# Two reorderings around the attentions of a transformer kernel: a gate's bank, a vector engine's order, four weight splits

## The chip, the cores and the metric

One core of one Trainium2 chip runs the whole program. The metric is the device time of one execution in microseconds. TensorE multiplies, VectorE (DVE) and ScalarE (ACT) work on tiles in SBUF and read the results of TensorE from eight PSUM banks of 128 x 512 float32, GpSimd (POOL) does a few small roots, and SyncE (SP) issues the transfers of the weights. Every engine works through its own instructions in order; they meet at semaphores only.

## The reference

Two transformer blocks on one sequence of 512 positions, width 1024, in float32. The first has a mixer of two halves (a gated linear attention and a latent attention with softmax), an MLP and a gated projection:

```python
o_g = gla_chunked(q_g, k_g, v_g, log_a)
o_g = rms_norm(o_g, gla_out_norm[i]).reshape(B, S, GLA_WIDTH) * jax.nn.silu(g_r)
o_m = mla_attention(q_m, k_m, v_m).reshape(B, S, MLA_WIDTH)
h = h + jnp.concatenate([o_g, o_m], axis=-1) @ w_out[i]
```

The second has a pooling mixer, a convolutional feed-forward network, a chunked attention of 16 heads, and the network again:

```python
qkv = h @ w_qkv
q, k, v = jnp.split(qkv, 3, axis=-1)
q = head_rmsnorm(q.reshape(B, S, N_HEADS, HEAD_DIM), q_norm)
k = head_rmsnorm(k.reshape(B, S, N_HEADS, HEAD_DIM), k_norm)
s = jnp.einsum('bqhd,bkhd->bhqk', qc, kb) * scale + bias[None]
p = jax.nn.softmax(s, axis=-1)
```

## The kernel before

**Products.** Each float32 product is made of three products of the faster kind: high part by high part, high by low, low by high (`triple`, L584 to L586, and `triple_t`, L590 to L592). So every unit of weights (128 x 2048) is loaded into a buffer `RAW` by SP, rounded into its high part `WH` by ACT (L1289, the split) and its low part `WL` is the difference, made by DVE (L1677). One unit of the first attention (`MIXED`, the first of the output projection) is split in four quarters on either engine (ACT L1420, DVE L1684), placed into steps of the attention.

**The first attention** (`tensor_program` from L771, `vector_program` from L1994) is a loop of 13 steps that each engine writes out in its own order. In step i TensorE makes scores of step i into banks 0 and 1 (L842), turns the weights of step i-2 into banks 4 and 5 (L852), multiplies the values of step i-3 into bank 6 (L867), turns heads (L771), then does some chunks of the gate projection (`gate_part`; the table `GATED` says how many in each step; 8 chunks are one tile, three products each), and last a level of the linear attention into banks 7 and 3 (L827). All four tiles of the gate go through bank 2, which DVE frees when it moves the tile into `gsil` (L2008). In steps 11 and 12 TensorE makes the states (`states`), for the second half of the heads into banks 0 and 1, and the output projection (`attended`, L896) follows.

DVE does in each step, in order: the finished gate tile, the level that is kept (L1929), the division of the last step's weights (L1975, L1980), the largest score of this step (L1991, L1997), in some steps the low part `LM` of the values (L2025, waits for ACT's `OM`), then the products with the decays (`decayed`) and the next decays' exponents (`decay`), and in steps 7 to 10 a quarter of `MIXED`.

**The second attention** is written out by one planner, `attend_order`, from which all engines take their steps. For each of the blocks of q and k TensorE multiplies the rows (`product`), two halves of the sum for each of four row groups q. After the second half ACT moves the result out of its bank and squares it (`z`, L1627, L1632), DVE sums and averages the squares (L2287, L2290), POOL takes the root (L2420), DVE scales the rows (`scale`, L2295, L2298), and two groups later TensorE turns them (`turn`, L1206) and ACT copies the turned tile out of bank 2 into `qTa` or `kTa` (L1637). The results of `product` go through banks 0 and 1 in turn, so the next but one product waits for ACT's `z`. The steps `high` (ACT's split of a unit, L1289) and `low` (DVE's, L1677) are placed by the same planner; the fourth of a block's two splits is placed at row group 2, second half, ahead of the turn:

```python
if done == 1:
    out.append(("sums", 5))
if (q, half) == (2, 1):
    high(u + 3)
if to_turn and to_turn[0][0] <= done - 3:
    out.append(("turn", *to_turn.pop(0)[1]))
```

The other split of a block, `high(u + 2)`, is placed at row group 1, first half, ahead of the product.

Of the kernel before, what the change touches and what calls it, by code (L numbers as in the profile page):

```python
# [15 lines left out]
P = 128  # L16
# [431 lines left out]
def attend_order():  # L448

    out, split, to_scale, to_turn = [], [], [], []
    pairs = [(0, 0), (1, 0), (0, 1), (1, 1), (2, 0), (3, 0), (2, 1), (3, 1)]
    groups = [(blk, q, half) for blk in BLOCKS for q, half in pairs]
    done = n = 0

    def high(u):
        out.append(("high", u))
        split.append(u)

    def low():
        while split:
            out.append(("low", split.pop(0)))

    def group():
        nonlocal done, n
        blk, q, half = groups[done]
        u = UNIT["qkv", 2 * blk]
        if (q, half) == (1, 0):
            high(u + 2)  # L470
        out.append(("product", blk, half, q))
        if done == 1:
            out.append(("sums", 5))
        if (q, half) == (2, 1):
            high(u + 3)
        if to_turn and to_turn[0][0] <= done - 3:
            out.append(("turn", *to_turn.pop(0)[1]))
        if half:
            if blk >= 4:
                out.append(("v", blk, q))  # L480
            else:
                out.append(("z", blk, q, n))
                to_scale.append((done, (blk, q, n)))
                n += 1
        while to_scale and to_scale[0][0] <= done - 1:
            at, piece = to_scale.pop(0)
            out.append(("scale", *piece))
            to_turn.append((at, piece))
        done += 1

    def project(m, i):
        if m % 4 == 0 and i == 0:
            high(UNIT["wo", 0] + m // 4 + 2)
        out.append(("part", m, i))

    for _ in range(20):
        low()
        group()
    steps, last = len(ATTEND), 11
    parts, tail = [(m, i) for m in range(8) for i in range(2)], steps + 2 - last  # L500
    for s in range(steps + 3):
        if 0 <= s - 1 < steps:
            out.append(("norm", s - 1))
        if s < steps:
            out.append(("scores", s))
        if 0 <= s - 2 < steps:
            out.append(("turned", s - 2))
        if s < steps:
            out.append(("largest", s))
        low()  # L510
        if 0 <= s - 3:
            out.append(("values", s - 3))
            if (s - 3) % 5 in (2, 4):
                out.append(("output", ATTEND[s - 3][0][0]))
        if s < steps:
            out.append(("weights", s))
        if s <= last:
            while done < 20 + 28 * (s + 1) // (last + 1):
                low()
                group()  # L520
        else:
            for m, i in parts[16 * (s - last - 1) // tail:16 * (s - last) // tail]:
                project(m, i)
                if i == 0 and m > 0:
                    out.append(("add", m - 1))
    out.append(("add", 7))
    return out
# [20 lines left out]
HEADS = {0: ((0, 2), (0, 3)), 1: ((1, 2), (1, 3)), 3: ((0, 4), (0, 5)), 4: ((1, 4), (1, 5)),  # L548
         5: ((0, 6), (0, 7)), 6: ((1, 6), (1, 7))}
LEVEL_AT = {1: 4, 2: 5, 3: 6, 4: 8, 5: 9, 6: 10}  # L550
GATED = {-1: 1, 0: 2, 1: 2, 2: 3, 3: 3, 4: 2, 5: 3, 6: 2, 7: 3, 8: 2, 9: 1, 10: 4, 11: 4}
STEPS1 = 10


def level_at(s):

    return next((lv for lv in LEVEL_AT if LEVEL_AT[lv] == s), None)
# [8 lines left out]
def tensor_program(k, e):  # L566
# [11 lines left out]
    def in_bank(b, *name):  # L578
        k.where[name] = b
        return MM.mark(*name)  # L580

    def triple(o, a, c, h, l, first, last):

        e.matmul(o, a, h, start=first, stop=False)  # L584
        e.matmul(o, a, l, start=False, stop=False)  # L585
        return e.matmul(o, c, h, start=False, stop=last)  # L586
# [188 lines left out]
    def gate_part(i):  # L775

        first = sum(GATED[x] for x in GATED if x < i)
        for n in range(first, first + GATED[i]):
            h, c = divmod(n, 8)
            u = UNIT["gr", h // 2]  # L780
            a, l = split_view(k, u, 8)
            cols = slice(h % 2 * P, h % 2 * P + P)
            if c == 0:
                w.wait_ge(WLO(u), *free[2])
            t = triple(bank[2][:, :], a[:, c, cols], l[:, c, cols], AH[:, c, :], AL[:, c, :], c == 0, c == 7)
            if c == 7:
                t.then_inc(*in_bank(2, "gr", h))
                free[2] = [DVE("gr", h)]
                MM.also("unit", u)

    def states(j):

        bs = ((3, 7), (0, 1))[j]
        w.wait_ge(ACT("kd", j))
        for c in (0, 2, 4, 6, 1, 3, 5):
            b = bs[c % 2]
            r0 = 64 * (c % 2)
            if c < 2:
                w.wait_ge(*free[b])
            for hh in range(2):  # L800
                h = 2 * j + hh
                t = e.matmul(bank[b][64 * hh:64 * hh + 64, (c // 2) * P:(c // 2 + 1) * P],
                             k.kd[r0:r0 + 64, c // 2, j * P + 64 * hh:j * P + 64 * hh + 64],
                             k.gv[r0:r0 + 64, c // 2, h * GV:(h + 1) * GV], start=True, stop=True, skip_group_check=True)
            if c in (5, 6):
                t.then_inc(*MM.mark("state", j, c % 2))
        free[bs[0]], free[bs[1]] = [DVE("state", j, 6)], [DVE("state", j, 5)]
# [86 lines left out]
    def attended(m):  # L894

        u = UNIT["wout", m // 4]  # L896
        a, l = split_view(k, u, 4)
        cols = slice(m % 4 * P, m % 4 * P + P)
        b = (3, 2, 0, 1)[m % 4]
        w.wait_ge(WLO(u), *free[b])  # L900
        for c in range(4):
            w.wait_ge(DVE("ol", 4 + c))
            t = triple(bank[b][:, :], a[:, c, cols], l[:, c, cols], k.OM[c][:, :], k.LM[c][:, :], c == 0, c == 3)
        t.then_inc(*in_bank(b, "res", 1, m))
        free[b] = [DVE("x", 1, m)]
        MM.also("unit", u)
# [757 lines left out]
def vector_program(k, e):  # L1664
# [291 lines left out]

    def chain(j):

        bs = ((3, 7), (0, 1))[j]
        for c in range(7):  # L1960
            o = bank[bs[c % 2]][:, (c // 2) * P:(c // 2 + 1) * P]
            w.wait_ge(MM("state", j, 0), MM("state", j, 1)) if c else w.wait_ge(MM("state", j, 0))
            if c == 0:
                w.wait_ge(MM("gr", 3))
                t = e.tensor_copy(k.ST[:, j, 0, :], o)
            else:
                w.wait_ge(DVE("state", j, c - 1), ACT("el"))
                t = e.scalar_tensor_tensor(k.ST[:, j, c, :], k.ST[:, j, c - 1, :], k.el[:, j, c:c + 1], o, MUL, ADD)
            t.then_inc(*DVE.mark("state", j, c))
# [13 lines left out]
    def largest(i):  # L1983
# [13 lines left out]
            t = e.scalar_tensor_tensor(k.st1[:, y:y + 2, x, 1], k.st1[:, y:y + 2, x, 0], -1.0, k.rn[:, 0, r:r + 2], MUL, MUL)  # L1997
        t.then_inc(*DVE.mark("neg1", i))

    zeros = cst[:, C_ZERO:C_ZERO + 1]  # L2000
    last()
    for i in range(STEPS1 + 3):
        h = gate_ends(i - 1)
        if h is not None:
            w.wait_ge(MM("gr", h))
            if h == 2:
                w.wait_ge(MM("level", 5, 1, 1))
            e.tensor_tensor(k.gsil[:, h, :], bank[2][:, :], rb[:, :], MUL).then_inc(*DVE.mark("gr", h))  # L2008
        if i == STEPS1 + 2:
            chain(0)  # L2010
        lv = level_at(i - 1)
        if i in (3, 4):
            keep(0, i - 3)
        elif lv:
            for j in range(2):
                keep(lv, j)
        if 0 <= i - 1 < STEPS1:
            divided(i - 1)
        if i < STEPS1:
            largest(i)  # L2020
        s = i - 3
        if s >= 0 and s % 5 in (2, 4):
            p = ATTEND[s][0][0]
            w.wait_ge(ACT("oh", 4 + p))
            e.tensor_tensor(k.LM[p][:, :], bank[6][:, :], k.OM[p][:, :].bitcast(F), SUB).then_inc(*DVE.mark("ol", 4 + p))  # L2025
        if level_at(i + 1):
            decayed(level_at(i + 1))
        if level_at(i + 2):
            decay(level_at(i + 2))
        if i == 0:  # L2030
            w.wait_ge(ACT("elast"), MM("gv", 1, 3))
            e.tensor_tensor(k.kt[0][:, :, :], k.gk[:, :, :], k.dd[:, :, :], MUL).then_inc(*DVE.mark("kdec"))
            split(9)
        if i == LEVEL_AT[6] + 1:
            w.wait_ge(ACT("efirst"))
            e.tensor_tensor(k.dd[:, :, :], k.gq[:, :, :], k.dd[:, :, :], MUL).then_inc(*DVE.mark("qdec"))
        if 7 <= i <= 10:
            quarter(MIXED, i - 7)

# [584 lines left out]
```

## Time and profile before

| | |
|---|---|
| median of 3 runs | 1654.26 us (1652.44, 1654.26, 1654.32) |
| profiled execution, its own time | 1654.58 us |
| its span, first to last instruction | 1652.8 us |
| TensorE busy | 1644.8 us (100% of the span as the page rounds it), 8124 products |
| DVE busy | 935.8 us (57%) |
| ACT busy | 615.6 us (37%) |
| POOL busy | 84.2 us (5%) |
| DMA | 94 GB/s mean, 25.4% of 16 engines' span for the weights' queue |
| TensorE's granted clock | 0.999 of full speed |

The chain that ended last is TensorE for 96% of the span. The first attention lies at about 95 to 182 us, the projection behind it runs to about 230 us, and the second attention lies at about 1043 to 1262 us.

### The profile page before, as it was taken

Reading aid. Unit: us, or ns where it says so; the run is one execution under the profiler, and the core shown is the slowest. Engines: PE = TensorE matmul, PEld = TensorE weight load, DVE = VectorE, ACT = ScalarE, POOL = GpSimd, SP = SyncE. Lnnn points to the kernel's source line nnn. Section 1 sums busy time; section 2 is a strip of 40 time slices with the busy share of each in tenths; the row PEclk is TensorE's granted clock in tenths of the full one; section 3 lists DMA queues with packets and bytes.
Section 4 is the critical chain, followed back from the end, with each engine's and each line's share of the span. In section 5 each row is a group of like instructions: output and inputs, shape, how many; then the busy total and the mean of one; then the engine's idle time right before and its main releaser. Section 6 shows DMA issues by size and latency. Waiting matters only on the chain.

```text
span 1652.8 us, 19172 instructions
## 1 busy us (share of the span) xinstructions
PE 1644.8 (100%) x8124; PEld 1341.9 (81%) x8124; DVE 935.8 (57%) x1379; ACT 615.6 (37%) x828; POOL 84.2 (5%) x80
## 2 busy tenths in 40 slices
PE   9999999999999999999999999999999999999999
PEld 7877878888888888888888888877777888888887
DVE  6797664434343546576456457546655577366353
ACT  5476444333232336433222223455655333122120
POOL 1300001000000000000000000311200100000000
PEclk9999999999999999999999999999999999999999
DMA  5210227445452521222322222322221222232311
GB/s 186 102 49 27 102 77 130 128 89 110 84 136 80 124 103 52 77 103 102 126 79 102 102 83 96 126 77 78 98 75 52 77 102 103 102 102 89 110 63 70
DMA packets 27909, 155.93 MB, mean 94 GB/s; under 512 B 3696, under 2 KB 5120, under 8 KB 11952
## 3 DMA queue, kind: packets, MB, share of 16 engines
q1 hardware_dynamic: 26352, 149.84, 25.4%
q0 software_dynamic: 1328, 4.86, 5.0%
q8 instruction: 64, 1.05, 0.3%
q14 instruction: 21, 0.17, 0.0%
q10 hardware_dynamic: 144, 0.00, 0.0%
HBM read 149.98 MB, written 4.72 MB: 94 GB/s over the span
## 4 chain that ended last, share of the span: by engine, by line
PE 96%; DVE 2%; ACT 1%; POOL 0%; DMA 0%; issue 0%; SPq 0%; DVEq 0%
PE bank L584 26%; PE bank L586 26%; PE bank L585 26%; PE bank L590 3%; PE bank L592 3%; PE bank L591 3%; PE bank L1218 1%; PE bank L1228 1%; PE bank L1244 1%; PE bank L842 1%; PE bank L827 1%; PE bank L1104 0%; PE bank L1206 0%; PE bank L771 0%; PE bank L867 0%; PE bank L606 0%
## 5 line engine op out<-in xcount | busy, mean ns | idle before, releaser
L584 PE MATMUL bank<-AH,WH 128*128 128x512 f32 (+1 forms) x1150 | 451.5, 393 | 1.5 <-DVE gsil L2008 1.4
L586 PE MATMUL bank<-AH,WL 128*128 128x512 f32 (+1 forms) x1150 | 447.8, 389 | 0.0
L585 PE MATMUL bank<-AL,WH 128*128 128x512 f32 (+1 forms) x1150 | 447.6, 389 | 0.0
L1677 DVE TENSOR_TENSOR WL<-RAW,WH 128x2048 fp32r<-128x2048 f32 (+1 forms) x133 | 298.5, 2247 | 192.7 <-ACT WH L1289 192.7
L1289 ACT ACTIVATE WH<-RAW 128x2048 fp32r<-128x2048 f32 (+1 forms) x133 | 248.3, 1871 | 259.3 <-PE bank L586 240.3
L584 PEld LDWEIGHTS bank<-AH,WH 128*128 128x128 f32 (+1 forms) x1150 | 215.5, 187 | 49.1 <-issue 2.4
L586 PEld LDWEIGHTS bank<-AH,WL 128*128 128x128 f32 (+1 forms) x1150 | 215.5, 187 | 45.9
L585 PEld LDWEIGHTS bank<-AL,WH 128*128 128x128 f32 (+1 forms) x1150 | 215.6, 187 | 45.6 <-issue 1.0
L584 PE MATMUL bank<-HH,WH 128*128 128x512 f32 x608 | 239.6, 394 | 0.0
L586 PE MATMUL bank<-HH,WL 128*128 128x512 f32 x608 | 238.4, 392 | 0.0
L585 PE MATMUL bank<-HL,WH 128*128 128x512 f32 x608 | 236.0, 388 | 0.0
L1707 DVE TENSOR_TENSOR X<-X,bank 128x512 f32<-128x512 f32 x112 | 76.6, 685 | 196.5 <-PE bank L586 196.3
L586 PEld LDWEIGHTS bank<-HH,WL 128*128 128x128 f32 x608 | 114.1, 188 | 26.8
L585 PEld LDWEIGHTS bank<-HL,WH 128*128 128x128 f32 x608 | 114.1, 188 | 25.5
L584 PEld LDWEIGHTS bank<-HH,WH 128*128 128x128 f32 x608 | 114.3, 188 | 22.8
L1598 ACT ACTIVATE t2s<-t2s,par 128x512 f32<-128x512 f32 x44 | 31.9, 724 | 186.7 <-DVE t2s L2253 186.7
L590 PE MATMUL bank<-WH,AH 128*128 128x512 f32 x224 | 90.0, 402 | 0.0
L592 PE MATMUL bank<-WH,AL 128*128 128x512 f32 x224 | 87.5, 391 | 0.0
L591 PE MATMUL bank<-WL,AH 128*128 128x512 f32 x224 | 87.3, 390 | 0.0
L1603 ACT ACTIVATE HH<-cvs 128x512 fp32r<-128x512 f32 x44 | 27.8, 632 | 126.0 <-DVE cvs L2259 126.0
L1518 ACT ACTIVATE t2s<-t1s 128x512 f32<-128x512 f32 x32 | 20.2, 632 | 97.4 <-DVE t1s L2148 97.4
L1296 ACT ACTIVATE sq<-X 128x512 f32<-128x512 f32 x49 | 30.9, 630 | 65.6 <-DVE X L1707 61.6
(306 smaller groups left out, 1746.0 us busy)
## 6 DMA issues: line engine op xcount, KB each, us to landing
RAW<-in_W SPq DMA_DIRECT2D x124, 1024.0 KB, 4.8
RAW<-in_W SPq DMA_DIRECT2D x9, 768.0 KB, 4.1
X<-in_XT SPq DMA_DIRECT2D x16, 256.0 KB, 5.8
ev_scratch<-ev POOLq DMA_DIRECT2D x16, 160.0 KB, 7.5
Gb<-ev_scratch SPq DMA_DIRECT2D x16, 128.0 KB, 2.9
out<-X SPq DMA_DIRECT2D x8, 256.0 KB, 2.0
Gb<-ev_scratch SPq DMA_DIRECT2D x16, 112.0 KB, 2.6
RAW<-in_W SPq DMA_DIRECT2D x2, 512.0 KB, 5.3
```

The source lines that it names most:

```text
L584: e.matmul(o, a, h, start=first, stop=False)
L585: e.matmul(o, a, l, start=False, stop=False)
L586: return e.matmul(o, c, h, start=False, stop=last)
L590: e.matmul(o, h, a, start=first, stop=False)
L591: e.matmul(o, h, c, start=False, stop=False)
L592: return e.matmul(o, l, a, start=False, stop=last)
L1289: e.activation(k.WH[SLOT_OF[u]][:, 0:n], k.RAW[RAW_OF[u]][:, 0:n], AF.Copy).then_inc(*WHI.mark(u))
L1296: e.activation(k.acc if j == 0 else sq[(j - 1) % 2][:, :], src, AF.Square).then_inc(*ACT.mark("sqr", n, j))
L1598: e.activation(t2s[i][:, :], t2s[i][:, :], AF.Silu, bias=par[:, PC_CB + 22 * l + m:PC_CB + 22 * l + m + 1]).then_inc(*ACT.mark("silu", l, m))
L1603: e.activation(k.HH[m % NH][:, :], k.cvs[i][:, :], AF.Copy).then_inc(*ACT.mark("hh", name, m))
L1677: e.tensor_tensor(k.WL[j][:, 0:n], k.RAW[RAW_OF[u]][:, 0:n], k.WH[j][:, 0:n].bitcast(F), SUB).then_inc(*WLO.mark(u))
L1707: e.tensor_tensor(X[:, m, :], X[:, m, :], src, ADD).then_inc(*DVE.mark("x", n, m))
```

## The change

In the first attention: the fourth tile of the gate (h = 3) goes into bank 0 in place of bank 2; the second half's states go into banks 2 and 1 in place of 0 and 1; the banks of the output projection are (0, 3, 2, 1) in place of (3, 2, 0, 1); `GATED` gives the stretch ahead of step 0 two chunks in place of one, and step 2 two in place of three; on DVE the third gate tile (h = 2) is moved out behind the division instead of at the start of its step, the low part `LM` comes behind `decayed` and `decay`, and the quarters 0 to 3 of `MIXED` are in steps 7, 10, 11, 11 in place of 7, 8, 9, 10. In the second attention the planner places the turn ahead of `high(u + 3)`; the two trade places wherever a turn is due there. No arithmetic changes.

```diff
         if done == 1:
             out.append(("sums", 5))
+        if to_turn and to_turn[0][0] <= done - 3:
+            out.append(("turn", *to_turn.pop(0)[1]))
         if (q, half) == (2, 1):
             high(u + 3)
-        if to_turn and to_turn[0][0] <= done - 3:
-            out.append(("turn", *to_turn.pop(0)[1]))
...
-GATED = {-1: 1, 0: 2, 1: 2, 2: 3, 3: 3, 4: 2, 5: 3, 6: 2, 7: 3, 8: 2, 9: 1, 10: 4, 11: 4}
+GATED = {-1: 2, 0: 2, 1: 2, 2: 2, 3: 3, 4: 2, 5: 3, 6: 2, 7: 3, 8: 2, 9: 1, 10: 4, 11: 4}
...
-            cols = slice(h % 2 * P, h % 2 * P + P)
+            cols, b = slice(h % 2 * P, h % 2 * P + P), 0 if h == 3 else 2
             if c == 0:
-                w.wait_ge(WLO(u), *free[2])
+                w.wait_ge(WLO(u), *free[b])
...
-        bs = ((3, 7), (0, 1))[j]
+        bs = ((3, 7), (2, 1))[j]
...
-        b = (3, 2, 0, 1)[m % 4]
+        b = (0, 3, 2, 1)[m % 4]
...
+    def gate_out(h):
+        w.wait_ge(MM("gr", h))
+        if h == 2:
+            w.wait_ge(MM("level", 5, 1, 1))
+        e.tensor_tensor(k.gsil[:, h, :], bank[where["gr", h]][:, :], rb[:, :], MUL).then_inc(*DVE.mark("gr", h))
...
+        if h is not None and h != 2:
+            gate_out(h)
...
             divided(i - 1)
+        if h == 2:
+            gate_out(h)
         if i < STEPS1:
             largest(i)
+        if level_at(i + 1):
+            decayed(level_at(i + 1))
+        if level_at(i + 2):
+            decay(level_at(i + 2))
         s = i - 3
         if s >= 0 and s % 5 in (2, 4):
...
-        if level_at(i + 1):
-            decayed(level_at(i + 1))
-        if level_at(i + 2):
-            decay(level_at(i + 2))
...
-        if 7 <= i <= 10:
-            quarter(MIXED, i - 7)
+        for x in {7: (0,), 10: (1,), 11: (2, 3)}.get(i, ()):
+            quarter(MIXED, x)
```

## Rows read from the trace of the kernel before

**Rows 1.** Waits of TensorE over the run: total us, times, longest.

```profile
PE bank L584 <- DVE gsil L2008: 1.4, 1, 1.4
...
PE bank L1206 <- ACT kTa L1637: 0.6, 1, 0.6
PE bank L842 <- ACT kT L1412: 0.6, 1, 0.6
PE bank L842 <- DVE st L1991: 0.4, 1, 0.4
...
PE bank L584 <- DVE ST L1968: 0.3, 1, 0.3
```

**Rows 2.** Timeline of TensorE, two neighbouring gate chunks: start us, us, instruction.

```profile
169.26 0.39 PE L584 MATMUL bank<-AH,WH 128*128 128x512 f32 x1
...
169.95 0.39 PE L584 MATMUL bank<-AH,WH 128*128 128x512 f32 x1
```

**Rows 3.** Timeline of DVE in the first attention, steps 7 to 10.

```profile
152.13 0.69 DVE L2025 TENSOR_TENSOR LM<-bank,OM 128x512 fp32r<-128x512 f32 x1 [3.00 <-ACT OM L1448]
...
161.31 0.69 DVE L1684 TENSOR_TENSOR WL<-RAW,WH 128x512 fp32r<-128x512 f32 x1
...
167.73 0.68 DVE L2008 TENSOR_TENSOR gsil<-bank,rb 128x512 f32<-128x512 f32 x1
```

**Rows 4.** Timelines of SP, ACT and DVE: the second unit of the output projection.

```profile
172.97 0.33 SPq L2443 DMA_DIRECT2D RAW<-in_W  x1
...
181.73 1.91 ACT L1289 ACTIVATE WH<-RAW 128x2048 fp32r<-128x2048 f32 x1
...
185.65 2.28 DVE L1677 TENSOR_TENSOR WL<-RAW,WH 128x2048 fp32r<-128x2048 f32 x1
```

**Rows 5.** Timeline of ACT in the second attention, first place of the exchange.

```profile
1054.85 1.91 ACT L1289 ACTIVATE WH<-RAW 128x2048 fp32r<-128x2048 f32 x1
1057.56 0.60 ACT L1637 ACTIVATE qTa<-bank 128x512 f32<-128x512 f32 x1 [0.81 <-PE bank L1206]
1058.06 0.68 ACT L1627 ACTIVATE qn<-bank,r 128x512 f32<-128x512 f32 x1
```

**Rows 6.** Timelines of DVE, POOL and TensorE behind the first place.

```profile
1060.24 2.28 DVE L1677 TENSOR_TENSOR WL<-RAW,WH 128x2048 fp32r<-128x2048 f32 x1
...
1064.05 0.69 DVE L2295 TENSOR_TENSOR qn<-qn,rn 128x512 f32<-128x512 f32 x1 [0.73 <-POOL rn L2420]
1064.78 0.69 DVE L2298 TENSOR_TENSOR qn<-qn,row 128x512 f32<-128x512 f32 x1
...
1060.41 5.21 POOL L2420 TENSOR_TENSOR rn<-mn,cst 128x8 f32<-128x8 f32 x2 [7.57 <-DVE mn L2290]
1072.26 1.64 POOL L2420 TENSOR_TENSOR rn<-mn,cst 128x8 f32<-128x8 f32 x1 [6.64 <-DVE mn L2290]
...
1060.14 0.39 PE L590 MATMUL bank<-WH,AH 128*128 128x512 f32 x1
...
1065.58 0.60 PE L1206 MATMUL bank<-cst,qn 128*128 128x128 f32 x4
```

**Rows 7.** Timelines at the third place (two rows) and the fourth (three).

```profile
1147.56 0.69 DVE L2298 TENSOR_TENSOR qn<-qn,row 128x512 f32<-128x512 f32 x1
...
1149.08 0.60 PE L1206 MATMUL bank<-cst,qn 128*128 128x128 f32 x4
...
1175.14 0.60 ACT L1637 ACTIVATE kTa<-bank 128x512 f32<-128x512 f32 x1
...
1187.99 1.90 ACT L1289 ACTIVATE WH<-RAW 128x2048 fp32r<-128x2048 f32 x1
...
1190.51 0.63 PE L1206 MATMUL bank<-cst,qn 128*128 128x128 f32 x4 [0.64 <-ACT kTa L1637]
```

**Rows 8.** Windows: engines' busy us (x instructions); the last but two is TensorE's clock.

```profile
196.00:200.00 4.00, 4.00 (x22) 3.49 (x23) 0.17 (x1) 3.74 (x5) 1.64 (x1) 0.79 0.00 0
200.00:204.00 4.00, 4.00 (x15) 3.17 (x15) 3.89 (x4) 0.08 (x1) 0.00 (x0) 0.78 0.15 16
```

More of the change, by code:

```diff
@@ L781, in gate_part @@
             a, l = split_view(k, u, 8)
-            cols = slice(h % 2 * P, h % 2 * P + P)
+            cols, b = slice(h % 2 * P, h % 2 * P + P), 0 if h == 3 else 2
             if c == 0:
-                w.wait_ge(WLO(u), *free[2])
-            t = triple(bank[2][:, :], a[:, c, cols], l[:, c, cols], AH[:, c, :], AL[:, c, :], c == 0, c == 7)
+                w.wait_ge(WLO(u), *free[b])
+            t = triple(bank[b][:, :], a[:, c, cols], l[:, c, cols], AH[:, c, :], AL[:, c, :], c == 0, c == 7)
             if c == 7:
-                t.then_inc(*in_bank(2, "gr", h))
-                free[2] = [DVE("gr", h)]
+                t.then_inc(*in_bank(b, "gr", h))
+                free[b] = [DVE("gr", h)]
                 MM.also("unit", u)
     def states(j):
-        bs = ((3, 7), (0, 1))[j]
+        bs = ((3, 7), (2, 1))[j]
         w.wait_ge(ACT("kd", j))
@@ L1957, in chain @@
     def chain(j):
-        bs = ((3, 7), (0, 1))[j]
+        bs = ((3, 7), (2, 1))[j]
         for c in range(7):
@@ L2003, in vector_program @@
         h = gate_ends(i - 1)
[L2004 to L2008, printed above, removed]
+        if h is not None and h != 2:
+            gate_out(h)
         if i == STEPS1 + 2:
```

## The prediction

> **What bounds the kernel now.** I read the views in this order. The page's busy shares and chain give TensorE 1644.8 us of a span of 1652.8 us and 96% of the chain: a change that leaves TensorE's work alone can only take away its waits, or add some. The list of TensorE's waits [rows 1] says how much there is to take: in the first attention 1.4 us for DVE's move of the third gate tile, 0.6 us for a head's copy ahead of the first scores, 0.4 us for the scores' bank and 0.3 us for the first tile of the output projection, 2.7 us together; in the second attention one wait of 0.6 us at a turn. That is 3.3 us in all, 0.2% of the time, and 0.2% (3.3 us) is also about what a measurement of this kernel tells from no change. So the change cannot be faster by a measurable amount unless TensorE's clock changes; the question is whether it adds waits. For that I went through the timelines of ACT, DVE, POOL and TensorE at each moved step, and asked how much time lies between a step's end and TensorE's need of it.
>
> **The first attention.** Four edits, each against one wait of [rows 1].
>
> The gate's chunks: one chunk is three products, 169.95 - 169.26 = 0.69 us [rows 2]. A second chunk ahead of step 0 fills the 0.6 us in which TensorE waits for the head's copy, and step 2 loses a chunk of the same length. TensorE's work is the same, the wait goes: -0.6 us. Step 0 comes 0.1 us later and step 2 ends 0.6 us earlier; at that point the largest score has been ready for a while and nothing is late next.
>
> The fourth gate tile in bank 0: TensorE waited 1.4 us because bank 2 is freed by DVE's move at 167.73 [rows 3], which stood behind two quarters of 0.6 us each (one is the row at 161.31). Bank 0 was read last by the largest score of step 9, before 166 us, so the tile starts at once: -1.4 us. The move of the third tile, now behind the division, has nobody waiting until the states' bank 2 in step 12, some 10 us later.
>
> The quarters moved from steps 8 and 9 to 10 and 11, and `LM` moved behind the decays: DVE's largest score of step 8 comes earlier. `LM` in step 7 had DVE idle for 3.00 us waiting for ACT's `OM` [rows 3]; `decayed` and `decay` (four operations of 0.6 us, 2.4 us) now go into that idle time, and `LM` starts at the same 152.1. The wait of 0.4 us for the scores' bank goes: -0.4 us. Behind `LM` is only bank 6 at the next values, a step away.
>
> The projection's first tile in bank 0: that bank is free after the fourth gate tile has been moved out, before `chain(0)` instead of behind it: -0.3 us.
>
> What the moved quarters push: the last quarter ends at about 175.7 instead of 172.9, and SP's load of the second unit of the projection, issued at 172.97 [rows 4], waits for it, with four loads of X queued behind it on SP. Loads took about 5 us to land. ACT's split of that unit was at 181.73, well after the landing; now, with TensorE 2.4 us earlier there, it would be wanted at 179.4 and can start at 180.6 to 182.6. DVE wants its high part where the row at 185.65 stands, 183.3 by the new clock: at worst 1.2 us late. TensorE needs that unit only at the fifth tile, more than 15 us later, so I cost this at nothing; without that cover it would be at most 1.2 us.
>
> Sum of the first attention: -(0.6 + 1.4 + 0.4 + 0.3) = -2.7; I take -2.6, since 0.1 us of a bank's wakeup tends to stay. Bounds: 0 (each wait replaced) and -2.7.
>
> **The second attention.** The exchange concerns ACT alone (on the other engines nothing stood between the two steps), and it happens at four places: the blocks' row group 2, second half, where a turn is due; at the two blocks of values none is. The remaining wait of 0.6 us is not among them: the copy `kTa` it waits for follows the split at 1187.99 [rows 7], which is a `high(u + 2)`, and that one is not moved.
>
> First place [rows 5]: ACT splits at 1054.85 for 1.91 us, is done 0.81 us before TensorE's turn is, then copies at 1057.56 and moves `z` at 1058.06. The split lay wholly in idle time. After the change ACT idles until 1057.56, copies, splits from 1058.06, and `z` follows one split later: 1.8 us (its 1.91 less the 0.1 by which ACT's instructions overlap in the records, as the copy's end at 1058.16 and `z` at 1058.06). So nothing is won at the turn, since the copy waits for TensorE anyway, and the `z` chain is later by 1.8 us. What hangs on it [rows 6]: DVE's sums, then its low part at 1060.24 for 2.28 us, the root on POOL, the scaling at 1064.05 and 1064.78, which ends at 1065.47; TensorE's turn of that tile starts at 1065.58. The slack is 0.1 us at best, and TensorE's preceding product leaves none. On the way TensorE also meets the bank: the product at 1060.14 needs the bank that `z` frees, now at about 1060.55, a wait of 0.4 us that counts inside the 1.8. The low part's high part is ready at 1059.97, ahead of DVE, so the order on DVE stays. Cost: 1.8 us. The second place repeats the first to 0.01 us, 23.7 us later: 1.8 us again.
>
> Third place: the same delay of 1.8 us goes through ACT's exponentials and DVE, which is busy without a gap there. The scaling ended at 1147.56 + 0.69 = 1148.25 and ends at 1150.05; TensorE's turn was at 1149.08 [rows 7]: 1150.1 - 1149.1 = 1.0 us.
>
> Fourth place: before, the split ended just as the turn was done, and `z` began 0.5 us after the copy at 1175.14 [rows 7]. Now 1.8 us later. The chain of the page runs from here over the square, the sums, two roots on POOL, the scaling, the division, the largest score, ACT's exponentials, the split at 1187.99 and the copy to the turn at 1190.51, which already waits 0.64 us: no slack, 1.8 us more. TensorE takes 0.4 us of it at the bank earlier.
>
> Sum: 1.8 + 1.8 + 1.0 + 1.8 = 6.4 us. Bounds: per place no less than the 0.4 us at the bank, no more than the split's 1.9 us: 1.6 to 7.6 us. I take 6.4, as the slack in each place is read from neighbouring rows.
>
> The root on POOL is where a rule could turn this. The pair of roots beside DVE's low part took 5.21 us, a root alone 1.64 us [rows 6]: the first was held for some 1.9 us while the low part ran. The Trainium skill says why (SBUF — State Buffer, section "Who interferes with whom"): a VectorE instruction with two SBUF inputs and a GpSimd one that reads SBUF exclude each other, and issue order decides who blocks. The trace agrees with the order that it needs: the low part starts at 1060.24, the root at 1060.41. By that rule the change would cost nothing at such a place if the root got in first.
>
> **Sum.** The profiled execution took 1654.58 us; 1654.58 - 2.6 + 6.4 = 1658.4. It lies 0.3 above the median of the runs, so I predict a median of 1658.1 us, 0.23% over 1654.26.
>
> **Rivals.**
> 1. The root runs ahead of the low part (not slower). If the high part of that unit came later than the averages are done (1062.0), DVE could not start the low part, the root would take 1.64 in place of about 3.6 us, and the 1.8 us would be swallowed at places 1 and 2 and in part at 4, leaving the bank's 0.4 us at each. It decides from a split that ends 2.1 us later than I place it. Time: 2 x 0.4 + 1.0 + 0.4 to 1.8 = 2.2 to 3.6, less 2.6: 1654 to 1655. Against it: the split ends at 1059.97 by duration of the row. The same time comes out if the planner's exchange leaves slack that I do not see. 0.14.
> 2. The clock. TensorE's granted clock is full everywhere but at 196 to 204 us, 0.79 and 0.78 [rows 8], the lower of the two levels (1.2 GHz) for part of it: 8 x 0.215 = 1.7 us lost. Just before it TensorE made 16 products of one column. The fastest run before is 1.8 us under the median, which fits a run without that dip. If the stretch, now shifted by 2.6 us, keeps full clock: 1656.4. 0.13.
> 3. More dips. TensorE's longest wait was 1.4 us and cost no clock. The fourth place now makes one of 0.6 + 1.8 - 0.4 = 2.0 us. A dip priced at 1.7 us from [rows 8] gives 1659.8. The Trainium skill (TensorE: Matmul & The Clock Gate, section "HAM oscillation — how this bites in real kernels") warns that waits between bursts of products let the clock fall; by that rule such dips would come at the longest of the new waits first, and no row here shows one behind a wait. 0.12.
> 4. The first attention's waits do not go but move (to the heads' copies, to bank 6): 1658.1 + 2.6 = 1660.7. For it: DVE is busy almost all of 156 to 172 us. Against it: the freed quarters give DVE 1.2 us there. 0.06.
>
> **Chances and range.** The forecast has 0.55. Its own range is 1657.2 to 1659.0 (the slack at each place is read to 0.1 or 0.2 us). Above 1657.6 (0.2% over the median) lie most of the forecast, rivals 3 and 4: 0.41 + 0.12 + 0.06, taken as 0.58 slower. Within 0.2% lie the rest of the forecast, rivals 1 and 2: 0.40. Faster by over 0.2% needs all waits gone and the dip too: 0.02. The range for 8 in 10 runs from 1654.6 (most of rival 1) to 1660.2 (rival 3).
>
> **What would show it.** Right: in the list of TensorE's waits the gsil wait and both L842 waits of the first attention gone; new waits for ACT's qn at L590 of about 0.4 us, and for DVE's qn at L1206 of 1.0 to 1.4 us, in the second attention; the wait for kTa near 2 us; ACT idle about 2.7 us ahead of the copies at L1637 with the split right behind. The distance from the second attention's start to its end longer by 6 us. Wrong: TensorE's L1206 rows without waits, the POOL pair shorter than 5.2 us, or a first attention that is no shorter.

## The result and the profile after

| | before | after |
|---|---|---|
| median (lowest to highest), 6 runs each, same chip | 1654.04 us (1652.44 to 1654.35) | 1659.70 us (1657.97 to 1659.88) |
| ratio, 95% interval | | 1.0031 [1.0021, 1.0041] |
| profiled execution, its own time | 1654.58 us | 1659.74 us |
| its span | 1652.8 us | 1657.6 us |
| TensorE busy | 1644.8 us | 1647.5 us |
| granted clock | 0.999 | 0.998 |

The kernel is slower by 0.31%, 5.2 us between the profiled executions. The prediction was 1658.1, with a range from 1654.6 to 1660.2.

One thing about the clock is needed to read all that follows. Every run has its granted clock, and the times fall into groups by it. In the five jobs of the experiments below the kernel before ran 89 times: 33 runs at clock 1.000 (mean 1652.70 us), 49 at 0.999 (1654.22), 6 at 0.998 (1655.69) and one disturbed run. Each step of 0.001 costs 1.5 us. The 14 profiles of this study show what it is. The four at 1.000 (e5, e7, e9, e11) have no dip. The six at 0.999 (before, e1, e3, e8, e10, e12) have one, like that of [rows 8], between 192 and 204 us. Of the four at 0.998, two (after, e4) have a second dip near 1194 us, and two (e2, e6) have a single one about twice as large. So a median says how long the kernel is and also how much it dipped. To know only the first, I compare runs of equal clock.

**TensorE's waits after** (total us, times, longest), to be held against [rows 1]:

```profile
PE bank L1206 <- DVE qn L2303: 1.9, 2, 1.0
PE bank L590 <- ACT qn L1627: 1.8, 4, 0.7
PE bank L1206 <- ACT kTa L1637: 1.8, 1, 1.8
PE bank L660 <- DVE rb L1729: 1.1, 1, 1.1
```

None of the four waits of the first attention is left. In their place stand seven in the second: two for the scaling, four at the banks that `z` frees, and the last turn's wait, 1.8 us where it was 0.6.

**ACT after, at the first place of the exchange** (start us, us, instruction, idle before), to be held against [rows 5]:

```profile
1054.31 0.60 ACT L1637 ACTIVATE qTa<-bank 128x512 f32<-128x512 f32 x1 [2.62 <-PE bank L1206]
1054.80 1.91 ACT L1289 ACTIVATE WH<-RAW 128x2048 fp32r<-128x2048 f32 x1
1056.61 0.68 ACT L1627 ACTIVATE qn<-bank,r 128x512 f32<-128x512 f32 x1
```

The copy waits 2.62 us for TensorE with nothing done in it, and `z` (L1627) starts 2.30 us behind the copy's start; before it was 0.50.

**POOL, DVE and TensorE behind it**, to be held against [rows 6]:

```profile
1058.95 5.21 POOL L2425 TENSOR_TENSOR rn<-mn,cst 128x8 f32<-128x8 f32 x2 [9.37 <-DVE mn L2295]
...
1058.78 2.28 DVE L1677 TENSOR_TENSOR WL<-RAW,WH 128x2048 fp32r<-128x2048 f32 x1
...
1063.32 0.69 DVE L2303 TENSOR_TENSOR qn<-qn,row 128x512 f32<-128x512 f32 x1
...
1056.66 0.39 PE L592 MATMUL bank<-WH,AL 128*128 128x512 f32 x1
1057.43 0.47 PE L590 MATMUL bank<-WH,AH 128*128 128x512 f32 x1 [0.38 <-ACT qn L1627]
1057.73 0.40 PE L591 MATMUL bank<-WL,AH 128*128 128x512 f32 x1
...
1062.73 0.39 PE L592 MATMUL bank<-WH,AL 128*128 128x512 f32 x1
1064.07 0.66 PE L1206 MATMUL bank<-cst,qn 128*128 128x128 f32 x4 [0.95 <-DVE qn L2303]
```

The chain is the one of the forecast: DVE's low part 0.17 us ahead of the root again, the pair of roots 5.21 us again, the scaling done at 1064.01, the turn at 1064.07. Read the starts as well as the wait in brackets. Products follow each other at 0.23 us. The one with 0.38 us of wait starts 0.77 us after its forerunner and its successor another 0.30: the stream is 0.6 us later, not 0.38.

**The third and the fourth place**, to be held against [rows 7]:

```profile
1147.55 0.50 PE L590 MATMUL bank<-WH,AH 128*128 128x512 f32 x1 [0.67 <-ACT qn L1627]
...
1150.48 0.65 PE L1206 MATMUL bank<-cst,qn 128*128 128x128 f32 x4
...
1193.76 0.63 PE L1206 MATMUL bank<-cst,qn 128*128 128x128 f32 x4 [1.80 <-ACT kTa L1637]
1194.31 1.81 PE L1218 MATMUL bank<-kTa,qTa 64*128 64x128 f32 x8
```

**Where the time went.** I took the same products of TensorE in both traces, and how far the distance between them changed:

| stretch | us |
|---|---|
| start of the kernel (a wait of 0.4 us at L640, 5 us into the kernel, is missing after; it was 0.9 us in e1, so it is not the change) | -0.4 |
| to the scores of step 3 (`GATED`) | -0.7 |
| to the scores of step 9 | -0.5 |
| to the states (fourth gate tile) | -1.4 |
| to the projection's tiles | -0.3 |
| exchange, places 1 to 4 | +1.75, +1.74, +1.03, +1.80 |
| second dip of the clock, 1194 to 1199 us | +1.7 |
| sum (of unrounded distances) | +4.8 |

The first attention gave 2.9 us, the exchange took 6.3. The dip is in the windows (us, then busy us of PE, PEld, DVE, ACT and POOL with the instructions, TensorE's clock, DMA share, GB/s). The first two are those of [rows 8], 4 us earlier; the last two are new:

```profile
192.00:196.00 4.00, 4.00 (x29) 3.56 (x28) 0.17 (x1) 3.32 (x5) 1.45 (x1) 0.82 0.00 0
196.00:200.00 4.00, 4.00 (x15) 3.15 (x14) 3.18 (x3) 0.79 (x1) 0.18 (x1) 0.76 0.00 0
...
1192.00:1196.00 4.00, 2.24 (x12) 1.08 (x12) 2.80 (x4) 2.79 (x4) 0.00 (x0) 0.83 0.01 4
1196.00:1200.00 4.00, 4.00 (x24) 3.25 (x23) 2.47 (x11) 2.48 (x6) 0.00 (x0) 0.74 0.80 293
```

### The profile page after: what moved, and what is told of

It is laid out like the page before. It is cut to its first block, busy times and chain, and to the rows that moved or that the text cites. A ratio compares the mean times of both kernels' runs of the same rounds, so it can differ in the third digit from the quotient of the medians.

```text
span 1657.6 us, 19171 instructions
## 1 busy us (share of the span) xinstructions
PE 1647.5 (99%) x8124; PEld 1342.3 (81%) x8124; DVE 936.0 (56%) x1379; ACT 615.7 (37%) x828; POOL 85.3 (5%) x80
## 4 chain that ended last, share of the span: by engine, by line
PE 97%; ACT 1%; POOL 1%; DVE 1%; DMA 0%; issue 0%; SPq 0%; DVEq 0%
PE bank L584 26%; PE bank L586 26%; PE bank L585 26%; PE bank L590 3%; PE bank L592 3%; PE bank L591 3%; PE bank L1218 1%; PE bank L1228 1%; PE bank L1244 1%; PE bank L842 1%; PE bank L827 1%; POOL rn L2425 1%; PE bank L867 1%; ACT WH L1289 1%; PE bank L852 1%; PE bank L771 0%
```

## The experiments

The changed kernel has two parts, and each part several edits. e1 and e2 separate the parts, e3 and e4 ask for the mechanism in the second, e5 to e7 take the first apart, e8, e9 and e11 try what the findings are good for, e10 and e12 ask about the second dip. All compute the whole reference.

### e1 and e2: each part alone

e1 is the changed kernel without the exchange, e2 the kernel before with the exchange alone:

```diff
+        if to_turn and to_turn[0][0] <= done - 3:
+            out.append(("turn", *to_turn.pop(0)[1]))
         if (q, half) == (2, 1):
             high(u + 3)
-        if to_turn and to_turn[0][0] <= done - 3:
-            out.append(("turn", *to_turn.pop(0)[1]))
```

> The changed kernel with the planner of before: only the first attention's edits. Theory (the cost lies in the second attention alone): TensorE's four waits of the first attention (1.4, 0.6, 0.4, 0.3 us) stay gone, the wait for kTa is 0.6 us as before, no waits for ACT's or DVE's qn; 2.8 us under the kernel before, ratio 0.9983, about 1651.3 us. Rival (part of the 5.6 us was made in the first attention, for instance by the later load of the projection's second unit): over 1653 us. One dip of the clock, near 193 us, as in both kernels.

> The kernel before with the planner's exchange alone. Theory (each place costs by itself: 1.75, 1.75, 1.0, 1.8 us): 6.3 us of new waits in TensorE's order; and if the second dip of the clock comes with the longest of them (1.8 us, for kTa), 1.7 us more: 1662.0 us, ratio 1.0048. Rival on the clock (the dip came only because the first attention moved the fourth place in time): no second dip, 1660.4 us, ratio 1.0038.

Measured: e1 1651.64 us (11 runs), ratio 0.9990 [0.9981, 0.9999]; e2 1661.08 us (5 runs), 1.0048 [1.0036, 1.0061]. At clock 0.999 e1 is at 1651.67, 2.5 us under the kernel before, and e2 at 1660.92, 6.7 us over it. The parts add up to half a microsecond: -2.5 + 6.7 = 4.2, and the changed kernel lies 3.7 us over the kernel before at that clock (e12, below); e2's figure rests on two runs. e2 has the long wait of 1.8 us too, and its clock is whole behind it (1.00 in the windows from 1196 to 1204 us): its 0.998 is one deep dip at 196 to 204 us. e2's list of waits has the new ones of after, to 0.1 us, beside all of [rows 1]:

```profile
PE bank L1206 <- DVE qn L2298: 1.9, 2, 1.0
PE bank L590 <- ACT qn L1627: 1.8, 4, 0.7
PE bank L1206 <- ACT kTa L1637: 1.8, 1, 1.8
PE bank L584 <- DVE gsil L2008: 1.4, 1, 1.4
```

So the loss is the exchange's alone and the first attention's waits went without moving elsewhere.

### e3: the fourth place undone

The edit is against the changed kernel.

```diff
+        if (q, half) == (2, 1) and blk == 3:
+            high(u + 3)
         if to_turn and to_turn[0][0] <= done - 3:
             out.append(("turn", *to_turn.pop(0)[1]))
-        if (q, half) == (2, 1):
+        if (q, half) == (2, 1) and blk != 3:
             high(u + 3)
```

> The changed kernel with the exchange undone at the fourth place only (block 3): there the split is ahead of the turn again. Theory: the wait for kTa is back at 0.6 us, one of the four waits of 0.4 to 0.7 us for ACT's qn at L590 goes, and the dip of the clock near 1194 us goes with the long wait: 1.8 + 1.7 = 3.5 us under the changed kernel, about 1656.2 us. Rival (the dip is not due to the wait): only 1.8 us less, about 1657.9 us, with a dip left somewhere in the second attention.

Measured: 1656.33 us (10 runs), ratio 1.0015 [1.0006, 1.0024]. At clock 0.999 it is at 1656.39 and the changed kernel at 1657.93 (8 runs, with e12): 1.5 us less; at clock 1.000 1654.55 (3 runs) against 1656.59 (3): 2.0. The place costs about its 1.8 us by itself. The median is 3.4 us under the 1659.70 of the first measurement, the number that was expected with the dip; but by the two differences at equal clock the place gives some 1.8 us of it, and the rest is how much each job dipped (e12). The last wait is back at 0.6 us and one of the four at the bank is gone.

### e4: the low part behind the root

A test of the mechanism on POOL: `low` is not placed ahead of the last step of a block's pass, so that DVE takes the averages of the tile first and the root has POOL's memory access for itself.

```diff
     for _ in range(20):
-        low()
+        if done % 8 != 7:
+            low()
         group()
```

> The changed kernel with the low part that follows z at places 1 and 2 moved behind the next scaling on DVE, so that the root on POOL runs with no low part beside it. Theory (the root is held for some 1.9 us by the low part, and that is part of the chain that makes TensorE wait): POOL's root 1.6 to 2.0 us in place of half of 5.2 and more, both waits for DVE's qn at L1206 (0.95 us each) gone, the 0.38 us for ACT's qn left: 1.9 us under the changed kernel. Rival (the root is slow for another reason, or the high part is what is late): the two waits stay within 0.2 us.

Measured: 1658.22 us (5 runs), ratio 1.0031 [1.0019, 1.0043]; at clock 0.999 1658.07, nothing under the changed kernel. The gain did not come, though the mechanism did what it was said to:

```profile
1059.10 3.24 POOL L2426 TENSOR_TENSOR rn<-mn,cst 128x8 f32<-128x8 f32 x2 [9.37 <-DVE mn L2296]
...
1062.11 2.29 DVE L1678 TENSOR_TENSOR WL<-RAW,WH 128x2048 fp32r<-128x2048 f32 x1
...
1063.10 0.60 PE L1207 MATMUL bank<-cst,qn 128*128 128x128 f32 x4
1064.45 0.50 PE L591 MATMUL bank<-WH,AH 128*128 128x512 f32 x1 [0.74 <-DVE WL L1678]
```

The pair of roots takes 3.24 us in place of 5.21, twice the 1.64 of one alone, and the turn at 1063.10 no longer waits. This is the Trainium skill's rule (SBUF — State Buffer, section "Who interferes with whom"): the two engines exclude each other at a shared port, and who comes first decides; here the trace agrees, 2.0 us for the pair. But the next product needs the low part, which now ends at 1064.4, and waits 0.74 us for it; over both places these waits are 1.5 us, where those for the scaling were 1.9. DVE has both the scaling and the low part to do ahead of that product; their order decides only which of the two is waited for.

### e5, e6 and e7: the first attention in pieces

Each is the kernel before with one group of edits, in one run each.

```diff
-GATED = {-1: 1, 0: 2, 1: 2, 2: 3, ...
+GATED = {-1: 2, 0: 2, 1: 2, 2: 2, ...
```

> The kernel before with the table GATED alone changed. Theory: the wait of 0.6 us for kT ahead of the first scores goes, the other three of the first attention stay (1.4, 0.4, 0.3 us); the distance from the first scores to the states is 0.7 us shorter. Rival: the wait moves to a later head or score.

e6 has the three moves of banks (fourth gate tile, states, projection), and DVE in its old order:

```diff
-            cols = slice(h % 2 * P, h % 2 * P + P)
+            cols, b = slice(h % 2 * P, h % 2 * P + P), 0 if h == 3 else 2
...
-        bs = ((3, 7), (0, 1))[j]
+        bs = ((3, 7), (2, 1))[j]
...
-        b = (3, 2, 0, 1)[m % 4]
+        b = (0, 3, 2, 1)[m % 4]
```

> The kernel before with the banks alone changed: fourth gate tile in bank 0, second states in 2 and 1, projection in (0, 3, 2, 1); DVE's order as before. Theory: the 1.4 us for gsil and the 0.3 us for ST go, the waits for kT (0.6) and for st (0.4) stay. The third tile's move is still ahead of the level that is kept, and the quarters are still there, so what is late next is at most DVE's level, which TensorE wants at 171.4 - 1.4: 0 to 0.5 us of a new wait at L827.

e7 has DVE's order alone (`LM` behind the decays, the quarters in steps 7, 10, 11, 11), all banks as before:

```diff
-        if 7 <= i <= 10:
-            quarter(MIXED, i - 7)
+        for x in {7: (0,), 10: (1,), 11: (2, 3)}.get(i, ()):
+            quarter(MIXED, x)
```

> The kernel before with DVE's order alone changed: the quarters in steps 7, 10, 11, 11 and LM behind the decays; the third gate tile's move stays at the start of its step, all banks as before. Theory: the 0.4 us for st at L842 goes, and the 1.4 us for gsil too, since DVE comes to that move some 2 us earlier; the waits for kT and ST stay. Rival: gsil stays at over 0.7 us, since its move also waits for level 5 of the linear attention, and then only the bank can take it away.

Measured, each against the kernel before at the same clock: e5 1652.14 us at 1.000, -0.55; e6 1655.18 at 0.998, -0.5; e7 1651.33 at 1.000, -1.4. These are one run each, and the runs of one kernel at one clock spread over some 0.7 us, so I rely on the waits. In e5 the wait for the head's copy is gone and the others stand. In e6 the waits for `gsil` and `ST` are gone, and a new one stands at the last level:

```profile
PE bank L827 <- DVE st L1975: 0.9, 1, 0.9
```

TensorE is early at the last level, and DVE, still with its quarters in steps 8 and 9, has not kept the level before. In e7 the waits for the scores' bank and, with it, the one of 1.4 us for `gsil` are gone: DVE moves the third tile at 164.59, 3.1 us earlier than in [rows 3]. A new wait stands in the projection, which fits the 1.4 us measured (0.4 + 1.4 - 0.4):

```profile
PE bank L940 <- DVE dg L2065: 0.4, 1, 0.4
```

By the waits the bank move alone gave 0.5 us of the 1.4 (1.4 less the new 0.9), and DVE's order alone took the whole wait away. My step "Bank 0 was read last by the largest score of step 9, before 166 us, so the tile starts at once: -1.4 us" named the wrong edit as the one that brings the 1.4 us.

### e8: the last wait

e1, and the split that stood between the exponentials and the last copy ([rows 7], 1187.99) put behind the turn:

```diff
-        if (q, half) == (1, 0):
+        if (q, half) == (1, 0) and blk != 5:
             high(u + 2)
...
             out.append(("turn", *to_turn.pop(0)[1]))
+        if (q, half, blk) == (1, 0, 5):
+            high(u + 2)
```

> The first attention's edits of the changed kernel, the planner of before, and one new edit: high(u + 2) of the last block of values (block 5), behind which the copy kTa stands, is placed behind the turn. Theory: the last wait of 0.64 us at the turn (L1206) goes, as ACT's copy comes 1.8 us earlier and nothing of q or k is squared behind it: 0.6 us under the kernel with the first attention's edits alone, at equal clock 1649.3 us without a dip and 1651.0 with one; ratio to the kernel before 0.998. Rival: ACT's later split makes v or the exponentials late, and a wait of 0.2 to 1.2 us comes at L590 or L1218.

Measured: 1650.91 us (11 runs), ratio 0.9982 [0.9973, 0.9991]; at clock 0.999 1650.84, 0.8 us under e1. The wait for `kTa` is gone. It is the same exchange as in the change, at a place where ACT was late for the copy and no `z` came behind the split.

### e10: the exchange at the fourth place alone

e1 with the turn ahead of the split in block 3 only, the mirror of e3 (the edit is against the changed kernel):

```diff
+        if (q, half) == (2, 1) and blk != 3:
+            high(u + 3)
         if to_turn and to_turn[0][0] <= done - 3:
             out.append(("turn", *to_turn.pop(0)[1]))
-        if (q, half) == (2, 1):
+        if (q, half) == (2, 1) and blk == 3:
             high(u + 3)
```

> The first attention's edits of the changed kernel, and the planner's exchange at the fourth place alone. Theory: 1.8 us over the kernel with the first attention's edits alone at equal clock (1649.9 without a dip, 1651.6 with one): 1651.7 and 1653.4 us; and the long wait of 1.8 us for kTa brings a second dip in about half of the runs, so some at 1655 us. Rival (the second dip needs the other three places too): no run with two dips but the odd one, as with the first attention alone (1 of 11).

Measured: 1653.38 us (11 runs), ratio 0.9999 [0.9990, 1.0008]; at clock 0.999 1653.48, 1.8 us over e1. The wait of 1.8 us stands at the last turn, but the clock stays whole behind it:

```profile
1192.00:1196.00 4.00, 4.00 (x23) 3.20 (x18) 2.69 (x12) 3.55 (x11) 0.00 (x0) 1.00 0.86 317
```

and 1 of 11 runs has the clock 0.998, where the changed kernel had 4 of 6. The long wait alone does not bring the dip each time, and not in about half of the runs, as the rival had it. Nor does 0.998 need the wait: e8, which has no wait at the last turn, is at 0.998 in 4 of 11 runs. That left two readings: the changed kernel dips because of something else in it, or the 4 of 6 were chance.

### e12: the changed kernel again

> The changed kernel once more, for the count of its dips. In its first six runs four had the granted clock 0.998 (two dips, or one of double length) and two had 0.999 (one); the kernel with the first attention's edits and the exchange at the fourth place alone (e10) had 0.998 in 1 of 11, with the same wait of 1.8 us there. The theory: the second dip belongs to the changed kernel as a whole (the long wait, met in a state that the earlier places bring about): then about 7 of 11 runs are at 0.998, the median is 1659.7 us and the profiled run shows, if it is one of these, a clock of about 0.8 in the two windows from 1192 to 1200 us again. The rival: the four of six were chance and the changed kernel dips as rarely as e10: then at most 3 of 11 runs are at 0.998, and the median is 1658.0 us. In both the runs at 0.999 lie at 1658.0 us, 3.8 us over those of the kernel before at 0.999.

Measured, in another job: 1657.83 us (10 runs), ratio 1.0024 [1.0015, 1.0034]. One run at 0.998 (1659.77), six at 0.999 (mean 1657.90), three at 1.000 (mean 1656.59): over the kernel before at the same clock 4.1, 3.7 and 3.9 us. The profiled execution has the same waits and no second dip:

```profile
1193.23 0.63 PE L1206 MATMUL bank<-cst,qn 128*128 128x128 f32 x4 [1.80 <-ACT kTa L1637]
1193.79 1.14 PE L1218 MATMUL bank<-kTa,qTa 64*128 64x128 f32 x8
```

L1218 takes 1.14 us here and took 1.81 in the first profile, behind the same wait of 1.80. So the exchange costs the same in both jobs (at 0.999 1658.01 us in the first, 1657.90 here), and the 1.9 us between the two medians are the clock's. The count, 1 of 10, is the rival's. That the first job's 4 of 6 were mere chance is not shown by it: none of that job's six runs of the kernel before lies near the 1655.7 us of clock 0.998.

The profiles say a little more. Five of them have the wait of 1.8 us at the last turn: after, e2, e4, e10 and this one. Two of the five show a dip behind it, after and e4:

```profile
1192.00:1196.00 4.00, 2.39 (x13) 1.18 (x14) 2.94 (x4) 2.64 (x4) 0.00 (x0) 0.82 0.01 4
1196.00:1200.00 4.00, 4.00 (x23) 3.24 (x23) 2.37 (x10) 2.63 (x7) 0.00 (x0) 0.75 0.92 302
```

None of the nine others dips there. So the dip was seen only behind the long wait, and not behind it every time. What makes a job dip often stays open; the kernel before too had 0.998 in 3 of 15 runs in one job and in none of 21 in another.

### e9 and e11: the dip at 196 us

[Rows 8] show the dip of the kernel before. Ahead of it TensorE goes through the products of the linear attention's outputs and then 16 one-column products, 5.4 us of narrow products in a row. e9 is e8 with a tile of the projection, 12 products of 512 columns, between the two groups of one-column products:

```diff
     out_sums(0)
+    attended(2)
     out_sums(1)
     free[7] = [DVE("mg", 0)]
-    attended(2)
     attended(3)
```

> The kernel e8_last_wait with one tile of the projection (attended(2), twelve wide products, 2.8 us) moved between the two sums of squares ahead of which, in all kernels so far, TensorE had made only narrow products for some 5.4 us (16 of 128 columns, 28 of 64, 16 of 1). Theory on the first dip (it follows that narrow stretch): no clock below full near 193 us, 1.7 us less than e8_last_wait in most runs, ratio 0.997. Rival (the dip has another cause): it stays in two thirds or more of the runs.

Measured: 1651.10 us (11 runs), ratio 0.9985 [0.9976, 0.9994]. All 11 runs have clock 1.000, and in the same job the kernel before dipped in 11 of 21. But the median is no better than e8's, since a wait has come:

```profile
PE bank L942 <- DVE dg L2072: 1.7, 1, 1.7
```

ACT's square of head 3 needs the buffer that the sums of head 1 read, which are now later; behind it stands the split of the projection's third unit, 3.1 us later than in e8. Its buffer, the load of the next unit, that unit's split, DVE's low part and the diagonal behind it follow:

```profile
197.23 0.63 ACT L1481 ACTIVATE sq<-AT 128x512 f32<-128x512 f32 x1 [3.03 <-PE bank L936]
197.77 1.90 ACT L1291 ACTIVATE WH<-RAW 128x2048 fp32r<-128x2048 f32 x1
206.92 1.91 ACT L1291 ACTIVATE WH<-RAW 128x2048 fp32r<-128x2048 f32 x1 [7.25 <-DMA RAW<-in_W]
...
208.86 2.29 DVE L1679 TENSOR_TENSOR WL<-RAW,WH 128x2048 fp32r<-128x2048 f32 x1 [2.47 <-ACT WH L1291]
```

e11 is e9 with that split ahead of the square:

```diff
         for hh in range(2):
             h = 2 * j + hh
+            if h == 3:
+                split(UNIT["wout", 2], MM("og", 3))
             w.wait_ge(ACT("og", h), ...)
             e.activation(sq[hh][:, :], k.AT[:, h, :], AF.Square)...
-    split(UNIT["wout", 2], MM("og", 3))
     split(UNIT["wout", 3])
```

> The kernel of e9 with ACT's split of the projection's third unit placed ahead of the square of head 3 (which waits for the sums of head 1, 3.03 us). The theory on e9: the clock's dip at 196 us is gone because a tile of full products now lies between the two groups of one-column products, and the gain was spent on a wait of 1.75 us at L942, which comes from the split of that unit 3 us late through its buffer, the load of the next unit and DVE's low part. By this the split starts at about 194.5 again, the wait at L942 goes to 0 to 0.1 us, no run shows a dip, and the median is 1649.4 us (1651.10 less 1.7), ratio 0.997 to the kernel before, 1.5 us under e8. The rival: the wait and the dip hang together (DVE's diagonal is late for another reason, its order behind attended): then the wait stays over 1 us and the median is 1650.5 to 1651.1. A second rival: the clock falls later in the stretch again once the wait is gone (the sums and the spreads come close together): wait gone, dips back in most runs, median 1650.8 like e8.

Measured: 1649.90 us (12 runs, 1648.84 to 1650.54), ratio 0.9974 [0.9964, 0.9983]. All 12 runs are at clock 1.000. The split starts at 193.67 and the wait is down to

```profile
PE bank L942 <- DVE dg L2073: 0.4, 1, 0.4
```

That is 1.2 us under e9 where I expected 1.7, most of the rest being these 0.4 us, and 4.1 us under the kernel before in the same job. At clock 1.000 it is 2.9 us under the kernel before (1649.80 to 1652.70) and 0.2 us under e8's two runs (1650.02), so what it gains over e8 is mainly that it does not dip. e11 is the fastest kernel of the study.

## Why the prediction came out as it did

**What bounds the kernel.** Right for the first attention: e1 won 2.5 us of the 2.7 that the list of waits held there. But 3.3 us "in all" was short. The full list of the kernel before has two more waits, both in its first microseconds, 1.1 us at L660 for DVE and 0.4 us at L640 for ACT; the change touches neither. And the clock's dip, 1.5 us in most runs, stands in no list of waits; e9 and e11 were without it in all runs.

**First attention, -2.6.** Measured -2.9 between the traces, -2.5 by e1 at clock 0.999. The 0.1 us held back for a bank's wakeup no run shows by itself. Term by term: `GATED` -0.7 for 0.6, scores' bank -0.5 for 0.4, gate tile -1.4 for 1.4, projection -0.3 for 0.3. The attribution of the 1.4 us to the bank was wrong (e6, e7), the sum was not touched by it, since both edits were made. The moved quarters cost nothing, as forecast: SP's load went out at 175.16, and ACT's split waited for it with nobody late behind, and still started 0.6 us before the earliest time forecast (180.6):

```profile
179.99 1.92 ACT L1289 ACTIVATE WH<-RAW 128x2048 fp32r<-128x2048 f32 x1 [1.18 <-DMA RAW<-in_W]
```

**Second attention, +6.4.** Measured +6.3, place by place 1.75, 1.74, 1.03 and 1.80 for 1.8, 1.8, 1.0 and 1.8; e2 gives 6.7 at clock 0.999. With the first attention the sum was +3.8, and at clock 0.999 the two kernels differ by 3.7. The reason for it held as well: the split had been in time in which ACT could do nothing else, and was moved into a chain without slack. Two details differ. At the third place I had the turn as the late one; the trace has a wait of 0.67 us at the bank, and the turn at 1150.48 follows right behind the scaling without a wait of its own. The two have the same 1.0 us between them. And the waits listed add up to 4.9 us more than before in the second attention (1.9 + 1.8 + 1.8 - 0.6), where the distance grew by 6.3: each interruption of the stream costs some 0.2 us beyond the wait in the list. I had worked from the delays on ACT and DVE, not from waits, and so was not misled by that.

**The rivals.** Rival 1: the root did not run ahead of the low part; its pair took 5.21 us again. Its price was wrong as well. e4 let the root go first, the pair fell to 3.24 us, and the time stayed (1658.07 for 1657.93 at clock 0.999): the rival counted the gain at the scaling and left out that TensorE's next product needs the low part, which then comes later. The waits of the first attention did not move. The dip at 196 us did not disappear in the profiled run, though it did in single runs (3 of e12's). Rival 3, a second dip at the fourth place, is what the first measurement shows: 1659.8 was its time, and 1659.70 the median. Its mechanism is only half right. The dip lay where it said, right behind the longest wait. But that wait is in both profiles of the changed kernel and in e10's, and 0.998 is the clock of only 5 of the changed kernel's 16 runs and of 1 of e10's 11. The Trainium skill (TensorE: Matmul & The Clock Gate, section "HAM oscillation — how this bites in real kernels") warns that waits between bursts of products let the clock fall; two profiles of one kernel, with the same wait of 1.80 us and L1218 at 1.81 and at 1.14 us, show that here it may come and may not.

**The term that was off** is the last one, from the sum to the median. I took the dips of the changed kernel to be those of the profiled execution before, one, and gave a second one 0.12. In the first job four of six runs were at 0.998, and the one that was profiled had two dips; in the second job one of ten was at 0.998. The forecast's 1658.1 us meets the second job's 1657.83 and lies 1.6 us, one step of the clock, under the first's 1659.70, which is outside the forecast's own range of 1657.2 to 1659.0. The wide range had room for it because rival 3 was in it: that the first median fell into the range is owed to a rival held unlikely, and which of the two medians one meets was luck.

## What to carry to other kernels

Before a step is put ahead of another on an engine, ask whether it stood in time in which the engine waits for someone else; then moving it behind gains nothing and delays all that follows, here by up to its whole length. Where a reordering gets rid of one wait, follow the engine that was the cause to what it does next: in e4 and e9 the same work showed up one consumer later, and the remedy in e11 was the one step of that chain that had no need to stand there. And where single microseconds count, sort the runs by their granted clock first; the difference between two kernels at equal clock was steady to 0.4 us between jobs, that of the medians was not.

## What the runs showed of the hardware

The clock's dips had not been expected to be a matter of chance. Behind 5.4 us of narrow products (16 of 128 columns, 28 of 64, then 16 of one column) the clock fell to its lower level (1.2 GHz of 2.4) for part of the next microseconds in 55 of the 88 undisturbed runs of the kernel before, taking each run below clock 1.000 as one of them, and the mean of such runs at 0.999 is 1.5 us longer. TensorE did not wait in that stretch; e7's profile has the same 5.4 us and no dip. In e8's trace the start of one product of 512 columns follows that of another at 0.43 us in the dip and at 0.23 outside:

```profile
195.78 0.63 PE L587 MATMUL bank<-LM,WH 128*128 128x512 f32 x1
196.21 0.63 PE L588 MATMUL bank<-OM,WL 128*128 128x512 f32 x1
...
197.65 0.40 PE L586 MATMUL bank<-OM,WH 128*128 128x512 f32 x1
197.88 0.39 PE L587 MATMUL bank<-LM,WH 128*128 128x512 f32 x1
```

With 12 wide products between the two groups of one-column products no run of 23 (e9 and e11) was below 1.000. A clock of 0.998 may be two dips, as in the first profile of the changed kernel, or one larger one: e2's has a single one, 0.55 and 0.60 in the windows from 196 to 204 us. Also new to me was the 0.2 us that an interruption of TensorE's stream costs beyond its listed wait: 0.38 us listed and 0.6 in the starts at the bank, 0.95 listed and 1.1 in the starts at the turn behind it (1062.73 to 1064.07, where a start follows the last at 0.23).
